# One gather of all assigned tokens in the expert layers of a two-layer encoder trunk

## The reference, cut to what matters

```python
SEQ, D_MODEL, N_EXPERTS, N_GROUPS, TOP_K, D_EXPERT = 256, 1024, 16, 4, 2, 512

def grouped_moe(xn, w_router, b_router, w_gate, w_up, w_down):
    xt = xn.reshape(256, 1024)
    scores = sigmoid(xt @ w_router)
    biased = scores + b_router
    # the best group of 4 experts, then the best 2 experts in it
    ...
    combine = one_hot(idx) * w          # 256 x 16, two non-zeros in a row
    y = 0
    for e in range(16):
        hdn = silu(xt @ w_gate[e]) * (xt @ w_up[e])      # 256 x 512
        y += combine[:, e:e+1] * (hdn @ w_down[e])       # 256 x 1024
    return y

h = h + g2 * grouped_moe(modulate(rms_norm(h, norm_ffn), sh2, sc2), ...)
```

## Time and profile before

| | |
|---|---|
| median of 3 runs | 962.38 us |
| the profiled execution | 962.2 us |
| its span, first to last instruction | 960.4 us |
| PE busy | 909.1 us, 95% |
| DVE busy | 378.8 us, 39% |
| ACT busy | 174.2 us, 18% |
| read from memory | 307.11 MB, 321 GB/s over the span |
| rounds of layer 0 | gate starts from 332.26 to 537.08 us |
| rounds of layer 1 | gate starts from 691.87 to 925.93 us |

### The profile page before, as it was taken

One profiled execution on the slowest core, in us unless ns is written; L12 is line 12 of the kernel. 1 busy time (PEld: TensorE's weight loads), 2 busy tenths in 40 slices (PEclk: granted clock), 3 DMA queues, 4 the chain that ended last, 5 costly groups with the idle time before them and its releaser, 6 DMA issues.

```text
span 960.4 us, 11800 instructions
## 1 busy us (share of the span) xinstructions
PE 909.1 (95%) x4455; PEld 489.8 (51%) x4456; DVE 378.8 (39%) x709; ACT 174.2 (18%) x318; POOL 37.0 (4%) x43
## 2 busy tenths in 40 slices
PE   3999999999998899999999988998899999999996
PEld 1688544444444454554545546864454554545542
DVE  3236768668823521223312342422521223322223
ACT  2000011121101302211112131331302212112211
POOL 0022100000001000000000002101000000000000
PEclk9799999999999999999999999999999999999999
DMA  9997899899649799699999974434199699089991
GB/s 343 391 398 282 332 364 389 333 380 379 265 175 392 308 386 416 270 424 420 422 422 422 407 291 175 176 132 173 46 393 421 268 424 418 2 351 422 423 376 44
DMA packets 61598, 308.63 MB, mean 321 GB/s; under 512 B 5991, under 2 KB 6122, under 8 KB 36222
## 3 DMA queue, kind: packets, MB, share of 16 engines
q1 hardware_dynamic: 59210, 304.42, 79.2%
q10 hardware_dynamic: 2356, 3.76, 1.1%
HBM read 307.11 MB, written 1.05 MB: 321 GB/s over the span
## 4 chain that ended last, share of the span: by engine, by line
PE 90%; DVE 5%; DMA 1%; ACT 1%; issue 1%; DVEq 0%; SPq 0%
PE bank L755 12%; PE bank L742 12%; PE bank L773 12%; PE bank L612 11%; PE bank L799 6%; PE bank L605 6%; PE bank L653 6%; PE bank L722 6%; PE bank L983 3%; DMA ring<-in_w_mod 1%; PE bank L765 1%; PE bank L938 1%; PE bank L499 1%; PE bank L521 1%; DVE y L1192 1%
## 5 line engine op out<-in xcount | busy, mean ns | idle before, releaser
L755 PE MATMUL bank<-ring,arena 128*64 128x256 f32 x1088 | 124.1, 381 | 0.0
L1251 DVE SCALAR_TENSOR_TENSOR part<-ring,cpad,part 128x1024 f32<-128x1024 f32 x84 | 110.0, 1309 | 21.5 <-DMA ring<-in_w_mod 16.3
L1473 DVE TENSOR_TENSOR arena<-bank,arena 128x256 f32<-128x256 f32 x34 | 21.1, 620 | 241.1 <-PE bank L755 241.1
L612 PE MATMUL bank<-ring,xnT 128*128 128x512 f32 x256 | 111.4, 593 | 0.0
L773 PE MATMUL bank<-ring,arena 128*64 128x512 f32 x480 | 108.9, 595 | 0.0
L742 PE MATMUL bank<-ring,arena 128*64 128x512 f32 x480 | 106.3, 595 | 0.6 <-DVE arena L1466 0.6
L755 PEld LDWEIGHTS bank<-ring,arena 128*64 128x64 f32 x1088 | 76.7, 137 | 46.8 <-issue 12.6
L612 PEld LDWEIGHTS bank<-ring,xnT 128*128 128x128 f32 x256 | 48.2, 190 | 60.5 <-issue 60.5
L722 PEld LDWEIGHTS bank<-arena,y 128*128 128x128 f32 x544 | 63.2, 192 | 12.3 <-DVE arena L1455 8.6
L722 PE MATMUL bank<-arena,y 128*128 128x128 f32 x544 | 63.7, 275 | 3.5 <-DVE arena L1455 3.5
L742 PEld LDWEIGHTS bank<-ring,arena 128*64 128x64 f32 x480 | 33.1, 137 | 63.2 <-issue 61.1
(11 more groups left out here) (241 smaller groups left out, 803.9 us busy)
## 6 DMA issues: line engine op xcount, KB each, us to landing
ring<-in_moe_w_up SPq DMA_DIRECT2D x64, 1024.0 KB, 9.1
ring<-in_moe_w_gate SPq DMA_DIRECT2D x56, 1024.0 KB, 9.3
ring<-in_moe_w_down SPq DMA_DIRECT2D x56, 1024.0 KB, 11.2
ring<-in_w_mod SPq DMA_DIRECT2D x48, 1024.0 KB, 12.5
ring<-in_ret_w_in SPq DMA_DIRECT2D x24, 1024.0 KB, 8.9
ring<-in_w_mod_kv SPq DMA_DIRECT2D x8, 1024.0 KB, 14.9
ring<-in_ret_w_out SPq DMA_DIRECT2D x8, 1024.0 KB, 9.1
arena<-in_moe_w_down SPq DMA_DIRECT2D x2, 2048.0 KB, 15.9
```

Source lines behind the costliest of these rows:

```text
L612: ins = pe.matmul(pair[tt][:], xnT[:, k, tok(tt)], w[:, k, :], start=(k == 0), stop=(k == KT - 1))
L755: ins = pe.matmul(bank[1 + f][e * 64:(e + 1) * 64, 0:256], xgT[:, k, e * 64:(e + 1) * 64], w(2 + e, k)[:, f * 256:(f + 1) * 256], start=(k ...
L1251: ins = dve.scalar_tensor_tensor(o, w[:, k, :], c, o, ALU.mult, ALU.add)
```

## The change

Only the first pair's rounds still gather for themselves (`rounds(..., gather=True)`), now into banks 0 and 1. Behind them, once in a layer, PE multiplies `y` by a 0/1 matrix `pick_all` of 256 x 512 (16 matmuls of 512 columns), so that all 512 assignments stand in consecutive columns, expert after expert, in `packed`; DVE and ACT evict the eight tiles in turn, with scale and shift. In every later round DVE copies 64 columns of `packed` for the first expert, from a start that it loads into a register, and ACT 64 for the second, into the same `xgT`.

For this, DVE computes in `locate` the start of each expert (`ends`), each token's two columns (`first_at`, `both_at`) and, for each possible round of an expert, the start as an integer (`starts`). GpSimd (POOL) builds `pick_all` from them by comparing a row of numbers 1 to 512 with each (`pick_every`). That row comes from memory by one more transfer on ACT's queue into `part`. `packed` shares its memory with `xnT`. PE's wait for the additions to `h` (`h_added`) moves from before gate to before the second half of up, since comb now writes banks 2 to 5. SP's program is not touched.

```diff
-                def rounds(begin, end, here, w):
+                def rounds(begin, end, here, w, gather=False):
                     with pe.Fori(begin, end) as u:
-                        pe.wait_ge(S["picked"], u * 2 + 1)
-                        for k in range(KT):
-                            for tt in range(TT):
-                                ins = pe.matmul(bank[4 + k // 4][:, (k % 4) * P:(k % 4 + 1) * P],
-                                                y[:, tt, k * P:(k + 1) * P], pick[:, tt, :],
-                                                start=(tt == 0), stop=(tt == TT - 1))
-                            if k % 4 == 3:
-                                ins.then_inc(S["gathered"], 1)
+                        if gather:
+                            pe.wait_ge(S["picked"], u * 2 + 1)
+                            for k in range(KT):
+                                for tt in range(TT):
+                                    ins = pe.matmul(bank[k // 4][:, (k % 4) * P:(k % 4 + 1) * P],
+                                                    y[:, tt, k * P:(k + 1) * P], pick[:, tt, :],
+                                                    start=(tt == 0), stop=(tt == TT - 1))
+                                if k % 4 == 3:
+                                    ins.then_inc(S["gathered"], 1)
                         pe.wait_ge(S["picked"], u * 2 + 2)
                         for tt in range(TT):
                             ins = pe.transpose(bank[6][:, tok(tt)], pickw[:, tt, :], ident)
...
-                        pe.wait_ge(S["h_added"], u * 4 + 4)
                         pe.wait_ge(S["xg_dve"], u + 1)
+                        if not gather:
+                            pe.wait_ge(S["xg_act"], u + 1)
...
                         up(0, range(KT)).then_inc(S["up_done"], 1)
+                        pe.wait_ge(S["h_added"], u * 4 + 4)
                         up(1, range(KT // 2))
...
-                rounds(0, bound(slice(1, 2), 1), here0, w0)
+                rounds(0, bound(slice(1, 2), 1), here0, w0, gather=True)
+                pe.wait_ge(pick_all_ready, TT * (l + 1))
+                for k in range(KT):
+                    if k >= 4:
+                        pe.wait_ge((packed_dve, packed_act)[k % 2], KT // 2 * l + (k - 4) // 2 + 1)
+                    for tt in range(TT):
+                        ins = pe.matmul(bank[(0, 1, 6, 7)[k % 4]][:], y[:, tt, k * P:(k + 1) * P], pick_all[:, tt, :],
+                                        start=(tt == 0), stop=(tt == TT - 1))
+                    ins.then_inc(packed_up, 1)
...
+                def locate():
+                    own.step(dve, dve.tensor_tensor_scan(ends[:], nil[:], cmp2[:, 2 * NE:3 * NE], 0.0, ALU.add, ALU.add))
+                    own.step(dve, dve.tensor_tensor(ends[:], ends[:], cmp2[:, 2 * NE:3 * NE], ALU.subtract))
+                    own.step(dve, dve.tensor_tensor(where[:], chosen[:], ends[:].unsqueeze(1).to_broadcast([P, TT, NE]), ALU.mult))
+                    own.step(dve, dve.scalar_tensor_tensor(where[:], place[:], 1.0, where[:], ALU.add, ALU.add))
+                    own.step(dve, dve.tensor_reduce(first_at[:], where[:], AX.X, ALU.max))
+                    own.step(dve, dve.tensor_reduce(both_at[:], where[:], AX.X, ALU.add))
+                    dve.tensor_tensor(both_at[:], both_at[:], first_at[:], ALU.subtract).then_inc(located, 1)
+                    for r in range(ROUNDS):
+                        dve.tensor_scalar(starts[l][:, r, :], ends[:], float(r * SLOTS), float(PACKED), ALU.add, ALU.min).then_inc(starts_ready, 1)
...
+                for k in range(0, KT, 2):
+                    dve.wait_ge(packed_up, KT * l + k + 1)
+                    dve.tensor_scalar(packed[:, k, 0:PACKED], bank[(0, 1, 6, 7)[k % 4]][:], scale[:, 1 + 2 * l, k:k + 1],
+                                      modc[:, MOD_COL[l] + 24 + k:MOD_COL[l] + 25 + k], ALU.mult, ALU.add).then_inc(packed_dve, 1)
+                dve.wait_ge(packed_dve, KT // 2 * (l + 1))
+                dve.wait_ge(packed_act, KT // 2 * (l + 1))
+                dve.wait_ge(pad_cleared, l + 1)
...
+                        at = dve.value_load(starts[l][0:1, bass.ds(again, 1), bass.ds(pair * 2, 1)], min_val=0, max_val=PACKED)
+                        dve.wait_ge(S["up_done"], u * 2)
+                        dve.tensor_copy(xgT[:, :, 0:SLOTS], packed[:, :, bass.ds(at, SLOTS)]).then_inc(S["xg_dve"], 1)
                         dve.wait_ge(S["slots_ready"], pair + u + 1)
+                        picks(u, pair)
                         into_h(u)
...
+            def pick_every(l):
+                pool.wait_ge(logit_parts, l + 1)
+                pool.memset(packed[:, :, PACKED:PACKED + SLOTS], 0.0).then_inc(pad_cleared, 1)
+                pool.wait_ge(located, l + 1)
+                pool.wait_ge(rank_in, 16)
+                for tt in range(TT):
+                    pool.tensor_scalar(pick_all[:, tt, :], rank_id, first_at[:, tt:tt + 1], None, ALU.is_equal).then_inc(one_picked, 1)
+                    pool.tensor_scalar(second, rank_id, both_at[:, tt:tt + 1], None, ALU.is_equal).then_inc(one_picked, 1)
+                    pool.wait_ge(one_picked, 2 * (TT * l + tt + 1))
+                    pool.tensor_tensor(pick_all[:, tt, :], pick_all[:, tt, :], second, ALU.add).then_inc(pick_all_ready, 1)
```

More of the change, by code:

```diff
@@ L164, in build_kernel @@
         slot_id = sb("slot_id", [P, SLOTS])
+        where = sb("where", [P, TT, NE])
+        first_at, both_at = sb("first_at", [P, TT]), sb("both_at", [P, TT])
+        ends = sb("ends", [P, NE])
+        starts = [sb(f"starts{l}", [P, ROUNDS, NE], I32) for l in range(2)]
+        nil = sb("nil", [P, NE])
         arena = sb("arena", [P, ARENA])
@@ new lines, in experts @@
+                with act.Fori(0, act.value_load(bounds[l][0:1, 1:2], min_val=1, max_val=ROUNDS * PAIRS)) as u:
+                    act.wait_ge(S["gathered"], u * 2 + 2)
+                    for j in range(4):
+                        k = 4 + j
+                        ins = A(xgT[:, k, :], bank[1][:, tok(j)], ACT.Identity,
+                                bias=modc[:, MOD_COL[l] + 24 + k:MOD_COL[l] + 25 + k],
+                                scale=scale[:, 1 + 2 * l, k:k + 1])
+                    ins.then_inc(S["xg_act"], 1)
+                    round_tail(u)
@@ L1098, in experts @@
+                with act.Fori(1, PAIRS) as pair:
+                    begin = act.value_load(bounds[l][0:1, bass.ds(pair, 1)], min_val=1, max_val=ROUNDS * PAIRS)
                     end = act.value_load(bounds[l][0:1, bass.ds(pair + 1, 1)], min_val=1, max_val=ROUNDS * PAIRS)
                     with act.Fori(begin, end) as u:
[L1101 to L1113, removed]
+                        again = nc.s_assert_within(u - begin, 0, ROUNDS - 1,
+                                                   skip_runtime_bounds_check_because="a pair has at most ROUNDS rounds")
@@ L1115, in _ @@
+                        at = act.value_load(starts[l][0:1, bass.ds(again, 1), bass.ds(pair * 2 + 1, 1)], min_val=0, max_val=PACKED)
+                        act.wait_ge(S["up_done"], u * 2)
+                        A(xgT[:, :, SLOTS:2 * SLOTS], packed[:, :, bass.ds(at, SLOTS)], ACT.Copy).then_inc(S["xg_act"], 1)
+                        round_tail(u)
             experts(0)
@@ new lines, in experts @@
+                locate()
+                dve.wait_ge(starts_ready, ROUNDS * (l + 1))
+                dve.wait_ge(S["comb_done"], 4)
+                dve.tensor_copy(slot_id[:], slots0).then_inc(S["slots_ready"], 1)
+                only = dve.value_load(bounds[l][0:1, 1:2], min_val=1, max_val=ROUNDS * PAIRS)
+                with dve.Fori(0, only) as u:
+                    dve.wait_ge(S["slots_ready"], u + 1)
+                    picks(u, 0)
+                    into_h(u)
+                    dve.wait_ge(S["gathered"], u * 2 + 1)
+                    for k in range(4):
+                        ins = dve.tensor_scalar(xgT[:, k, :], bank[0][:, tok(k)], scale[:, 1 + 2 * l, k:k + 1],
+                                                modc[:, MOD_COL[l] + 24 + k:MOD_COL[l] + 25 + k], ALU.mult, ALU.add)
+                    ins.then_inc(S["xg_dve"], 1)
+                    round_tail(u)
@@ L1450, in experts @@
                     with dve.Fori(begin, end) as u:
-                        dve.wait_ge(S["slots_ready"], pair + u + 1)
[L1453 to L1456, removed]
-                                          ALU.is_equal).then_inc(S["picked"], 1)
```

98 lines of the change are left out of this document (66 added, 32 removed).

## The result

The changed kernel takes 978.74 us (median of 4 runs) against 962.33: 1.69% slower, ratio 1.0169 (95% interval 1.0156 to 1.0182). The forecast was 968.6 with a range up to 977. Direction right, size outside the range. The profiled execution took 978.23 us with a span of 976.4, so the difference to explain is 976.4 - 960.4 = 16.0 us, of which the prediction had 6.2.

The account below looks back on a forecast made before the run. Before, PE and transfers were both full, PE never waiting; after, the transfer queue was to bind layer 0. Layer 0 +8.5 and layer 1 -2.3 gave +6.2 us, so 968.6, range 961.5 to 977.

Parts of the forecast that it names:

- 5.9 us to spare in the queue: Layer 0 before the change: the last ups land at 538.2, PE needs them at 544.1.
- a restart fixed by round 2: SP's queue in layer 0 restarts at round 2's `up_done`, forecast 14.4 us later, at 419.7.
- the end of layer 0 set by the ups of pair 7: Ups land at 552.6, 132.9 us behind the restart; PE waits for them; layer 0 +8.5 us.
- B: Gather of all on PE between round 0's comb and round 1: 16 matmuls, 13.93 us, nothing hidden.
- The hole's place: Behind the gather of all, before round 1's gate: PE stands 5.0 us for eviction, loads, copy, products and weight turning.
- `pick_all` in time: POOL builds it in 8 us, or 14 if stretched; needed 32 us later, so hidden.
- Round 1: Its gate in layer 0 starts at 378.6, against 361.58 before: 17.0 us later.
- C: The hole behind the gather of all, in which PE stands: 5.0 us, bounds 3.5 and 8.
- A: `locate`, once a layer, on the path to the first gather: +2.0 us a layer, bounds 0.5 and 4.
- D: Head of a later round: PE waits 0.9 us at each new pair, bounds 0.2 and 2.0; period 26.6.
- Layer 1: From first gate to last comb, 255.2 us predicted against 259.5 before, with no wait for the ups.
- Rival 3: Dearer round heads: new register loads cost 0.9 or more, POOL holds DVE up; 979.5 us, chance 0.17.

Follow-up runs that it names:

- e6: Changed kernel with the weight loads behind pair 0 bringing half of each gate and up piece, 8 MB a pair for 12: 970.76 us.
- e7: Kernel before the change with the same half pieces of gate and up, 8 MB a pair for 12: 963.57 us against 962.94.
- e1: Changed kernel with six unused 512-column matmuls on PE in the hole behind the gather of all, once a layer: 973.96 us.
- e2: e1 with three more filler matmuls ahead of each layer's first gather and two more at the start of the MLA stage: 971.83 us.
- e9: Kernel before plus the gather of all in layer 1 alone, both copies on ACT, filler matmuls in the hole and before the first gather: 957.17 us against 962.94.
- e10: Changed kernel with both copies on ACT and filler matmuls in the hole and before the first gather, in both layers: 970.25 us.
- e3: Changed kernel with ACT making both 64-column copies and both loads of `starts`, DVE none: 975.24 us.
- e4: Changed kernel with the gather of all in layer 1 alone; layer 0 gathers each round and has no `locate`: 967.45 us against 963.12 before.
- e8: Changed kernel with the 16 matmuls of the gather of all moving 64 columns instead of 512: 956.80 us.

## Why the prediction was wrong

**Right.** The bound was read right: 5.9 us to spare in the queue, a restart fixed by round 2, the end of layer 0 set by the ups of pair 7 (landed 133.5 after the restart, forecast 132.9); e6 and e7 show it. B, 13.93 forecast and 13.75 measured. The hole's place and its releaser. `pick_all` in time. Round 1 within 0.4 us of its forecast.

**The step that failed** is the one that priced gate behind the hole at its steady 7.02 us. I counted C as 5 us in which PE stands, and said nothing of how fast PE is afterwards. Four places on the path are slower at a lower granted clock than their rows of before: the gates behind the two holes (+2.06 and +2.55), layer 1's first gather (+1.62) and MLA's first matmuls (+1.78), 8.0 us of the 9.8 that the forecast lacks. For the two gates e1 shows the cause; for the first gather e2, e9 and e10 do, as far as five fast ones out of five can; for MLA it was only seen. The 8.0 and the sizes below leave some tenths, as A came out lower than forecast. Each gate of the kernel before follows other matmuls within 0.3 us, and a price taken from a row holds only for an operation that starts as that row's did. The trace of before did hold the sign elsewhere, in PE's work ahead of the router of each layer:

```profile
309.25 1.09 PE L499 MATMUL bank<-cst,y 128*128 128x128 f32 x8 [3.41 <-DVE y L1192]
311.09 1.97 PE L499 MATMUL bank<-cst,y 128*128 128x128 f32 x8 [0.74 <-DVE y L1192]
...
669.15 3.65 PE L499 MATMUL bank<-cst,y 128*128 128x128 f32 x16 [3.39 <-DVE y L1192]
```

After 3.4 us in which PE stood still the granted clock went to 0.50 (from 310.7 to 314.1, and from 669.1 to 672.5), and the same eight matmuls took 1.97 us for 1.09. So this could have been priced before the result.

**Sizes.** D: 0.9 forecast, 1.14 measured (e3), as the third load with its register work is 1.02 and not 0.6: +0.24 at a new pair, about 1.2 in layer 1 and 0.2 in layer 0, where the queue covers the rest. C: 5.0 forecast, 5.7 measured in each layer (0.2 of it the turning of the weights at the lower clock). A: +2.0 forecast; without the clock +1.0 in layer 0, and 0.4 to 0.6 in layer 1 (e9). The meeting with POOL did happen, but was cheap:

```profile
326.79 1.57 POOL L1688 TENSOR_SCALAR part<-part,first_at 128x512 f32<-128x512 f32 x1 [11.36 <-DVE both_at L1493]
327.04 0.49 DVE L1537 COPY slot_id<-cst 128x64 f32<-128x64 f32 x1
...
328.34 1.66 POOL L1689 TENSOR_SCALAR part<-part,both_at 128x512 f32<-128x512 f32 x1
328.61 0.80 DVE L1514 TENSOR_TENSOR arena<-arena,combine 128x256 f32<-128x256 f32 x1
```

The slot copy took 0.49 for 0.20 and the second product 0.80 for 0.42, while the first took 0.43 as ever; the sum is 0.7, as I had it, but only the product that PE does not wait for first was hit, so it lay beside the gather. The Trainium skill ("SBUF — State Buffer", on the shared port pair) would have an operation blocked for the rest of the other's instruction; the trace does not bear a full block out. The two stretched ones ended 0.8 and 0.6 us ahead of the end of the POOL pass beside them (at 327.53 and 329.41, the passes at 328.36 and 330.00), and in layer 1 both products took 0.42 beside such passes. The measurement decides.

**Layer 1.** Forecast -4.3, measured +0.1: 2.6 of the 4.4 is the slow gate, 0.6 the hole, 1.2 the heads. So the gain of this layer was real and was spent on the hole; e9 got it back.

Rival 3 ("the head is dearer") named a total near the measured one, 979.5, but for another cause: D was 1.14, not 1.6, and C 5.7, not 7.

## What to carry to other kernels

Where PE and the transfers are both full, work saved on PE is worth only what the queue has in hand, and a block of PE work put early delays every later request: ask when the queue restarts, before counting what is saved. A stretch in which PE stands still can cost twice, once itself and once in the matmuls behind it, unless PE is given something to do; look in the trace at hand for matmuls behind such a stretch and at their granted clock. When a change trades many small costs for one large one, the place of the large one decides: here the change is 1.7% slower in both layers, 0.3% slower in layer 1 alone, whose queue had slack (e4), and 0.7% faster there with the hole filled and both copies on ACT (e9).

## What the runs showed that was not expected

After PE had stood still for 5.0 us (3.8 in e3), a gate of 7.02 us took 8.7 to 9.7 in each of the nine holes left open (two in the changed kernel, e3, e6 and e8, one in e4), at granted clocks of 0.77 and 0.73 in the changed kernel; with matmuls in the gap it took 7.02. After gaps of 0.9 us in each round it did not happen once. Between the two it was uneven. Of thirteen waits for the ups of 2.2 to 3.9 us, seven were followed by ups of 6.7 to 8.3 us and six, with 2.2 to 3.7 us, by the usual 5.40 (2.73 and 2.77 in e8 cost nothing, 2.77 in the changed kernel 1.7). What decides between them is not shown. The Trainium skill ("TensorE: Matmul & The Clock Gate", "Why this matters for your kernels") warns of idle gaps between bursts of matmuls, after which the array is back at half clock; the nine holes agree, with 1.7 to 2.7 us as the price of one such gap. Two register loads on DVE cost 1.22 us at the head of a round, and the load of `starts` with its index work 1.0: at the head of a loop that PE waits for, three of them outweigh the copy of 64 columns (0.43).
